# A two-layer hybrid decoder trunk on one core: which weight units are split in two, how the router counts, and where the norm's gain is applied

## The reference

```python
for i in range(2):
    hn = rms_norm(h, attn_norm_g[i])
    u = hn @ w_in[i]                     # conv | z | xbc | dt, cq, ckv, krope
    y = concat(conformer_conv(...),      # 31 taps per channel, group norm, silu
               ssd_mixer(...),           # Mamba-2, chunks of 128, gated group norm
               mla_mixer(...))           # 4 heads of attention
    h = h + y @ w_out[i]
    hn = rms_norm(h, ffn_norm_g[i])
    if i == 0: h = h + (silu(hn @ wg) * (hn @ wu)) @ wd
    else:
        logits = hn @ router             # 8 experts
        top_val, top_idx = top_k(logits, 2); gates = softmax(top_val)
        h = h + sum over the 2 experts of gate * swiglu(hn, expert)
    gate = sigmoid(rms_norm(h, ple_norm_g[i]) @ ple_w_gate[i])
    h = h + (p[i] @ ple_w_proj[i]) * gate
return rms_norm(h, final_norm_g)
```

## Time and profile before

| | |
|---|---|
| median of 3 runs | 1562.33 us |
| profiled execution | 1562.21 us, its span 1560.3 us |
| layer 0 mixers and output projection, 18.7 to 138.6 us | PE busy 95.0 of 98.0, then 21.9 of 21.9 |
| dense feed-forward, 148.5 to 382.4 us | PE busy 233.9 of 233.9 |
| embedding 0, 382.4 to 420.4 us | PE busy 31.8 of 38.0 |
| layer 1 mixers, 425.4 to 523.4 us | PE busy 96.6, DVE 72.2, ACT 46.1 of 98.0 |
| router to first expert product, 545.2 to 576.4 us | PE busy 16.9, DVE 18.0 of 31.2 |
| experts, 576.4 to 1514.2 us | PE busy 908.5, DVE 831.6, ACT 733.5 of 937.8; 377 GB/s |
| embedding 1 and last norm, 1514.2 to 1560.3 us | PE busy 32.7 of 46.1 |

### The profile page before, as it was taken

One profiled execution on the slowest core, in us unless ns is written; L12 is line 12 of the kernel. 1 busy time (PEld: TensorE's weight loads), 2 busy tenths in 40 slices (PEclk: granted clock), 3 DMA queues, 4 the chain that ended last, 5 costly groups with the idle time before them and its releaser, 6 DMA issues.

```text
span 1560.3 us, 18290 instructions
## 1 busy us (share of the span) xinstructions
PE 1476.0 (95%) x6932; PEld 1193.4 (76%) x6932; DVE 1187.5 (76%) x1106; ACT 1014.8 (65%) x947; POOL 9.3 (1%) x21
## 2 busy tenths in 40 slices
PE   6999999999899969999999999999999999999987
PEld 5767888887777758887778887778887778887766
DVE  2796455544468768989998979998979998979984
ACT  3465444434426547768887768887768887778874
POOL 0000000000000000000000000000000000000000
PEclk9999999999999979999999999999999999999998
DMA  8435555555241059999999999999999999999970
GB/s 294 136 108 185 184 185 185 181 187 176 81 155 35 1 216 408 368 339 392 392 395 390 367 352 377 390 394 397 356 355 382 385 396 394 369 345 379 389 280 28
DMA packets 143670, 441.80 MB, mean 283 GB/s; under 512 B 6928, under 2 KB 21296, under 8 KB 143584
## 3 DMA queue, kind: packets, MB, share of 16 engines
q1 hardware_dynamic: 142832, 438.24, 76.1%
q0 software_dynamic: 752, 2.39, 0.4%
HBM read 439.56 MB, written 1.05 MB: 282 GB/s over the span
## 4 chain that ended last, share of the span: by engine, by line
PE 75%; DVE 13%; ACT 7%; issue 5%; DMA 0%; DVEq 0%; ACTq 0%; SPq 0%
PE psum L509 16%; PE psum L511 16%; PE psum L510 16%; DVE w_lo L1661 9%; PE psum L548 5%; ACT w_hi L1224 5%; PE psum L946 4%; PE psum L947 4%; PE psum L562 3%; PE psum L990 2%; PE psum L530 1%; PE psum L905 1%; PE psum L914 1%; PE psum L984 1%; DVE hidden_a L1667 1%
## 5 line engine op out<-in xcount | busy, mean ns | idle before, releaser
L1661 DVE TENSOR_TENSOR w_lo<-ring,w_hi 128x2048 fp32r<-128x2048 f32 x396 | 900.2, 2290 | 244.8 <-ACT w_hi L1224 243.8
L1224 ACT ACTIVATE w_hi<-ring 128x2048 fp32r<-128x2048 f32 x396 | 755.7, 1916 | 285.8 <-PE psum L511 251.1
L511 PE MATMUL psum<-w_hi,hidden_b 128*128 128x512 f32 x560 | 219.2, 391 | 0.0
L946 PE MATMUL psum<-w_hi,xT_parts 128*128 128x512 f32 x448 | 193.3, 432 | 10.9 <-DVE w_lo L1661 10.8
L509 PE MATMUL psum<-w_hi,hidden_b 128*128 128x512 f32 x448 | 178.5, 398 | 7.3 <-DVE w_lo L1661 7.3
L947 PE MATMUL psum<-w_lo,xT_parts 128*128 128x512 f32 x448 | 175.7, 392 | 0.0
L510 PE MATMUL psum<-w_lo,hidden_b 128*128 128x512 f32 x448 | 175.1, 391 | 0.0
L509 PE MATMUL psum<-w_hi,hidden_a 128*128 128x512 f32 x352 | 138.8, 394 | 5.4 <-DVE hidden_a L1667 5.4
L509 PE MATMUL psum<-w_hi,xT_parts 128*128 128x512 f32 x352 | 138.5, 394 | 5.1 <-DVE xT_parts L1668 2.8
L510 PE MATMUL psum<-w_lo,xT_parts 128*128 128x512 f32 x352 | 137.7, 391 | 0.0
L510 PE MATMUL psum<-w_lo,hidden_a 128*128 128x512 f32 x352 | 137.7, 391 | 0.0
(11 more groups left out here) (308 smaller groups left out, 1640.3 us busy)
## 6 DMA issues: line engine op xcount, KB each, us to landing
ring<-in_moe_w_gate SPq DMA_DIRECT2D x112, 1024.0 KB, 7.2
ring<-in_moe_w_up SPq DMA_DIRECT2D x112, 1024.0 KB, 7.6
ring<-in_moe_w_down SPq DMA_DIRECT2D x112, 1024.0 KB, 7.3
ring<-in_w_in SPq DMA_DIRECT2D x16, 1024.0 KB, 5.3
ring<-in_dense_w_gate SPq DMA_DIRECT2D x14, 1024.0 KB, 5.1
ring<-in_dense_w_up SPq DMA_DIRECT2D x14, 1024.0 KB, 5.1
ring<-in_dense_w_down SPq DMA_DIRECT2D x14, 1024.0 KB, 4.9
ring<-in_w_out SPq DMA_DIRECT2D x8, 1024.0 KB, 4.9
```

Of the source, the lines that this page charges most:

```text
L511: return mm(o, a[1], b[0], start=False, stop=final)
L946: mm(o, xl_hi_lo[kt], w[0][:, q, c], start=kt == 0, stop=False)
L1224: A(part(w_hi, g, sizes[g]), raw(g, sizes[g]), ACT.Copy).then_inc(hi_ready, 1)
L1661: V.tensor_tensor(part(w_lo, g, sizes[g]), raw(g, sizes[g]), f32(part(w_hi, g, sizes[g])), ALU.subtract).then_inc(lo_ready, 1)
```

## The change

1. `RAW_IN`: of the ten input units of a layer only 0, 6, 7, 8 and 9 stay exact; 1 to 5 are split. `take_xT` therefore makes the exact and the split input both, and `conv_taps` is cut at other places.
2. The router works in plain fp32, token by token, with the exact transposed input. `rstd` is no longer in the logits but in the exponent of the gates and in the selection matrices.
3. The rank sums are three products of 24 columns.
4. The rows `xs` are made where the output projection is added to `h`, with the gain alone. The gain's broadcast is in the mixers of layer 1, by ACT and PE.
5. In the embedding the transposes of `h` come ahead of the embedding's products, and DVE takes the embedding ahead of the last experts' rows.
6. At the first expert the splits come between the two halves of the gathered input, PE waits for each half by itself, and SP reads the loop's count after the first three pairs.

```diff
-IN_UNITS = 10
+RAW_IN = (0, 6, 7, 8, 9)
-        EXACT = [g < IN_UNITS or N0 - NF <= g < N0 - NF + IN_UNITS for g in range(N0)]
+        EXACT = [g in RAW_IN or g - (N0 - NF) in RAW_IN for g in range(N0)]
...
             def channels_by_tokens(key, b):
+                exact = EXACT[len(last_reader)]
...
-                        wait_xT(kt)
-                        last = mm(o[:, m * SEQ:m * SEQ + SEQ], w[:, kt, m * P:m * P + P], xT[:, kt, :],
-                                  start=kt == 0, stop=kt == KT - 1)
+                        if exact:
+                            if m == 0:
+                                wait_exact(key[1], kt)
+                            last = mm(o[:, m * SEQ:m * SEQ + SEQ], w[:, kt, m * P:m * P + P], xT[kt],
+                                      start=kt == 0, stop=kt == KT - 1)
+                        else:
+                            wait_xT(kt)
+                            last = product(o[:, m * SEQ:m * SEQ + SEQ], at(w, ALLP, kt, slice(m * P, m * P + P)),
+                                           at(xTp, ALLP, kt), kt == 0, kt == KT - 1)
...
                 last.then_inc(banks.is_full(("pv", L)), 1)
+                if L == DEPTH - 1:
+                    pe.wait_ge(gain_diag, 1)
+                    for half, b in enumerate((3, 1)):
+                        o = banks.fill(pe, ("gain", half), b)
+                        mm(o, ones, gain_diag_f[:, half * 512:half * 512 + 512], start=True, stop=True).then_inc(
+                            banks.is_full(("gain", half)), 1)
...
                         scatter(n_iter - 1, 1, n, True, True)
+                ple_x(L)
                 pe.wait_ge(*banks.taken(("pT", L)))
...
+            lg = [banks.fill(pe, ("lg", t), 4 + t) for t in range(NT)]
             for kt in range(KT):
                 wait_xT(kt)
-                last = product(o[0:NE, 0:SEQ], at((rt_hi, rt_lo), ALLP, kt), at(xTp, ALLP, kt), kt == 0, kt == KT - 1)
+                for t in range(NT):
+                    last = mm(lg[t][:, 0:NE], xr[kt][:, t * P:t * P + P], rt_v[:, kt, :], start=kt == 0, stop=kt == KT - 1)
...
+            mm(o[:, 0:3 * NE], tri, counted[:, 0:3 * NE], start=True, stop=False)
+            mm(o[:, 0:3 * NE], ones, counted[:, 5 * NE:], start=False, stop=False)
+            mm(o[:, 0:3 * NE], ones, counted[:, 2 * NE:5 * NE], start=False, stop=True).then_inc(
...
-                if r == 0 and u == 0 and ch == 0:
-                    pe.wait_ge(xg_free, xg_done(i, k, 1 - k))
+                if u == 0 and ch == 0 and r in ((0,) if k else (0, 2)):
+                    pe.wait_ge(xg_free, xg_done(i, k, r // 2))
```

On ACT and DVE (the mixers of layer 1, the router, the first expert):

```diff
                 A(st, o, ACT.Copy).then_inc(banks.is_free(("st", L)), 1)
+                if L == DEPTH - 1:
+                    for kt in range(KT):
+                        last = A(gain_diag_f[:, kt * P:kt * P + P], ident, ACT.Copy, scale=lp(L, "g_ffn", kt))
+                    last.then_inc(gain_diag, 1)
+                    for half in range(2):
+                        o = banks.filled(act, ("gain", half))
+                        A(gain_of[half], o, ACT.Copy).then_inc(banks.is_free(("gain", half)), 1)
                 warm_up()
                 act.wait_ge(ygz_ready, L + 1)
...
+                    for t in range(NT):
+                        last = A(ev[:, t:t + 1], dv[:, t:t + 1], ACT.Exp, scale=rstd[:, t:t + 1])
...
+                    take_heavy(0, 0)
+                    split(N0)
+                    split(N0 + 1)
+                    take_heavy(0, 1)
+                    split(N0 + 2)
...
+                conv_taps(0, 1)
+                split(f + 4)
+                conv_taps(1, 8)
+                split(f + 5)
...
-                conv_taps(26, CK)
+                conv_taps(24, CK)
...
                         V.tensor_tensor(v, v, o, ALU.add).then_inc(banks.is_free(("o", L, t, half)), 1)
+                        if L == DEPTH - 1:
+                            dve.wait_ge(*banks.taken(("gain", half)))
+                            dve.wait_ge(*banks.taken(("o", L, t, half)))
+                            V.tensor_tensor(xs[:, t, half * 512:half * 512 + 512], v, gain_of[half], ALU.mult)
...
-                for half in range(2):
-                    o = banks.filled(dve, ("gain", half))
-                    c = slice(half * 512, half * 512 + 512)
-                    for t in range(NT):
-                        last = V.scalar_tensor_tensor(out=xs[:, t, c], in0=h[:, t, c], scalar=rstd[:, t:t + 1], in1=o,
-                                                      op0=ALU.mult, op1=ALU.mult)
...
+                        last = V.tensor_scalar(sel[:, t, 0:n], iota[:, 0:n], column(slot_of, t, i, k),
+                                               rstd[:, t:t + 1], ALU.is_equal, ALU.mult)
```

More of the change, by code:

```diff
@@ L1277, in take_xT @@
                     o = banks.filled(act, (("n", k), b))
+                    if k % 3 == 0 and b % 2 == 0:
+                        for q in range(2):
+                            last = A(xT[2 * b + q], o[:, q * SEQ:q * SEQ + SEQ], ACT.Copy,
+                                     scale=lp(L, gain, 2 * b + q))
+                        last.then_inc(exact_by_act, 1)
+                    elif k % 3 == 0:
+                        act.wait_ge(exact_by_dve, 2 * L + b // 2 + 1)
                     for q in range(2):
@@ L1430, in _ @@
                     norm(3 * L, h_added, squared=2)
-                take_exact_xT(3 * L, L)
+                take_xT(3 * L, L, "g_attn")
+                for g in range(1 + L, 4):
+                    split(L * (N0 - NF) + g)
                 mixers(L)
```

228 lines of the change are left out of this document (110 added, 118 removed).

## The result

The changed kernel takes 1548.24 us (median of 4 runs, 1546.86 to 1551.26) against 1562.55 for the kernel before in the same runs: a ratio of 0.9912, 95% interval 0.9893 to 0.9930. 1549.0 was forecast. The profiled execution took 1549.22 us, its span is 1547.4.

What follows compares the result with a forecast made beforehand. PE was taken to set the pace in the mixers, the experts to run on PE, ACT and DVE with DMA ahead. -4.4 - 1.0 - 6.6 - 1.2 - 1.0 + 1.0 = -13.2 on 1562.21 us gave 1549.0; range 1545 to 1555.

Steps and rivals of the forecast that it cites:

- The products: Mixers on PE, each layer: five units as fp32r products take 26.3 us instead of 32.6, saving taken as 6.2.
- The rival by which the weight load shows: Mixers: 128-column weight load not hidden beneath 256 columns; at 0.235 us each 1582 us; chance 0.05, shared with other stalls.
- DVE's room: Mixers, gated input to `acs`: DVE's busy time 45.1 us fits a window shrunk to 46.3, 1.2 us over.
- take over: Rival in the mixers: DVE's small waits or a late split push everything behind; up to 4.5 us lost, 1553.5; chance 0.17.
- Layer 1's gain: End of layer 1's mixers: ACT's gain copies and table load decide, squares start 1.0 us earlier instead of 4.4; -1.0.
- The clock in layer 1: PE stands about 4 us behind layer 1's gain products and returns at lower clock: +1.0 us, could be 0 or 1.5.
- The dense layer: Between layer 0's mixers and layer 1: no term in the sum, forecast change 0.
- The router: Router to first expert product: PE starts the experts at 569.8 instead of 576.38, -6.6 us.
- five products took 2.41, three take 1.5, so 0.9 is gained: Router's rank sums: time from rank products to DVE's reading falls from 2.41 us to 1.5.
- The rows and the split of expert 0: Before expert 0: row products of 2.72 us leave the gather's path; ACT splits the first half at once; within the -6.6.
- the DMA takes the gain back: Rival at the experts' start: loads set the pace, only their earlier issue counts, 2.9 for 6.6 us; 1552.7; chance 0.12.
- The embeddings: Transposes ahead of products need only the third addition: -1.2 us in layer 0, -1.0 at the kernel's end.

Runs made afterwards that it cites:

- second experiment: Changed kernel with ACT's two copies of the gain's broadcast moved behind its squares and the last split of layer 1's mixers: 1542.82 us, ratio 0.9870.
- last kernel: Changed kernel with later gain copies, earlier Exp table, last embedding's transposes behind its products, plus unread products in two PE waits: 1539.81 us, ratio 0.9858.

## Why the prediction was right, point by point

The forecast was 1549.0 and the result 1548.2; the sum was -13.2 and the spans give -12.9. Its largest steps held; several smaller ones were wrong inside, and chance and errors that cancel brought the sum back to 0.3 us.

- **The products.** 0.119 and 0.191 us were read from the earlier trace rows; 0.120 and 0.192 were measured, 26.7 us for five units instead of 26.3. The rival by which the weight load shows is out: 0.235 would have been seen. Layer 0 gave -4.5 for -4.4, and two errors cancel in it: undoing the products costs 5.6 us and not the 6.2 booked, and with them undone layer 0 is 1.1 us longer than before, where the two late taps were booked at 1.8.
- **DVE's room.** It did not take over, but the reading was off: the prediction took all 6.2 us out of the window from the gated input to `acs`, although unit 1 lies before that window. It shrank to 48.00 us and not to 46.3; DVE's busy time, 44.86, was booked well at 45.1. So 3.1 us of room were left, not 1.2.
- **Layer 1's gain.** Booked -1.0 instead of -4.4, because ACT must wait for the gain's broadcast; measured -0.7. ACT's squares came 0.7 us earlier, counted from the layer's first unit, for the 1.0 booked. The second experiment, which moves two copies and nothing else, gives 3.7 us back. This was the best founded of the steps.
- **The clock in layer 1.** Booked +1.0, between nothing and 1.5. Measured +1.8: a size that was off. The bound of 1.5 came from one start of the experts; ten records in 4 us at 0.52 cost more than eleven at 0.57.
- **The dense layer.** Not in the sum, and -1.6. The step that failed is the silent one, that a stretch whose instructions do not change keeps its time. In the fourteen profiles of this study PE waits the same 2.8 us there (0.56 in the last kernel); in six it comes back at 0.50 to 0.61, in eight at 1.00. Nine of the other kernels run the changed kernel's code up to that product; five of them start it at 1.00 and four at 0.50 to 0.61. So I call it chance. It was luck for the forecast: it covered the 0.8 of layer 1 and the 0.6 us by which this execution started later.
- **The router.** -6.4 for -6.6, with two errors inside that cancel. The step "five products took 2.41, three take 1.5, so 0.9 is gained" failed: the ranks were no longer what DVE waited for, ACT's late table load was. The change itself had moved that load behind a second wait, which the prediction did not look at, since no activation was added. Undoing it gives 0.7 us of order, and with it the three products count 0.8. On the other side the logits were 0.4 us quicker than booked.
- **The rows and the split of expert 0.** Both had been booked as if they were needed for the 6.6. The order of the split is worth 0.8 us to the end (1.9 at equal clock), the place of the rows 1.4 at the first product. At the last scatter nothing of that was left in the one execution, by a clock that may be chance. The 6.4 us at the first product can be bettered by the 0.8 of the early table. Beyond that the loads come near: the first splits already wait for them (the first for 0.79 us), and with the clock up such waits cost PE 1.2 us more. The rival "the DMA takes the gain back" had its mechanism right. It did not bite here: in the slow first 4 us PE ran eleven products, under one unit, while a load came every 2.6 us.
- **The embeddings.** -1.2 and -1.0 were forecast and -1.2 and -1.1 measured, but the reason given for the second was wrong. The prediction had PE's transposes need the third addition, and gain by standing first. The experiment shows that they lose 1.4 us by it; DVE's rest, made before the additions, is what gained. The sum had also left out what the clock behind the old wait cost there (7.16 us for 5.57). The changed kernel did not get it back, since its transposes ran at half clock instead. In layer 0 the transposes in front are worth 2.4 within the changed kernel, not 1.2: without them PE waits 1.50 us for the split embedding, as in the earlier trace rows, and 0.88 more for a split weight that was not late before the change.

## What to carry to other kernels

When a value is made earlier so that a later stage gets it for nothing, look at the queue of the engine that has to copy it: two copies of 0.6 us placed one line too early cost 3.7 us and the clock behind them, by the last scatter 4.4 us, a third of what the whole change won. An activation table may be loaded behind the waits of its first use, so look in the trace where the load stands after every change to that use; one dummy use in front moved it here. And a part that is undone in an experiment tells its worth only in its own stretch of the timeline, since a debt elsewhere can hide it in the whole. So can the clock: a term of 1 or 2 us needs the granted clock of its stretch beside it.

## What was not expected of the hardware

The granted clock behind a short wait is not fixed by that wait's length. Behind the same 2.79 us of idle time PE started the dense layer at 1.00 in seven profiles and at 0.50 to 0.61 in six, where it costs 1.5 to 2.8 us (271.7 us to layer 1's transposes at full clock, 273.2 at about 0.6, 274.5 at 0.50). In the one profile with products that nobody reads in the wait it was at 1.00, and the transposes of layer 1, at 0.57 for 4 us in the changed kernel, ran in 3.84 us for 5.47. The clock also fell where PE had not just stood. In the second experiment PE had run without a stop since the projection's first product, 25 us before, and its logits, products of 8 columns behind transposes, took 4.75 us for 3.64; the stretch from 540.5 to 542.5, inside them, shows 0.50.
